# First attention in pairs of heads, with one 512-column bias product per head and the outputs split between two engines

## The chip, the cores and the metric

One core of a Trainium2 chip runs the whole program. The metric is the device time of one execution in microseconds (us); the kernel before took 2679.9 us (median of three runs, 2677.56 to 2681.17). The engines named here: TensorE (PE in the profile, PEld for its weight loads) multiplies into eight PSUM banks; VectorE (DVE), ScalarE (ACT) and GpSimd (POOL) do elementwise work; SyncE (SP) issues DMAs. Each engine works through its own queue in order and waits on semaphores.

## The reference, cut to what matters

The program is a transformer block (`first_block`) followed by two layers of another kind. Only the attention part of `first_block` is touched. It has 8 MoBA heads of 64 (with 256 tokens there is one block, so this is causal attention), 8 sliding-window heads of 64 that share 2 key/value heads, and 4 memory heads of 128:

```
s = q @ k.T * scale + bias_table[h, bucket(qpos - kpos)]      # MoBA and window heads
s = where(allowed, s, -inf)
p = exp(s - max(s)); p = p / (sum(p) [+ exp(sink - max)])     # the sink only for window heads
o = p @ v                                                     # 256 tokens x 64 (or 128)
merged = sigmoid(g_mb)*(o_mb @ w_branch_moba) + sigmoid(g_sw)*(o_sw @ w_branch_swa) + sigmoid(g_me)*(o_me @ w_branch_mem)
```

Memory heads have no bias and no mask. Everything is float32.

## The kernel before, in words

**A split-product kernel.** Every weight matrix is streamed by DMA in blocks into `raw` (two buffers), split by ACT into `w_hi` and by POOL (line 749) into `w_lo`, and used by PE (line 1934) in three products, hi by hi, hi by lo and lo by hi. Each of these buffers has two slots, so the split of a block waits until PE has used up the block two before it. Activations too are kept as a rounded part and a rest (`u_hi`/`u_lo`, `o1_hi`/`o1_lo`).

**The first attention** (step `att1` of the plan) runs over 20 units `UNITS1`: 8 MoBA heads, 8 window heads, 4 memory heads. A unit's scores are 256 queries by 256 keys and lie in one PSUM bank: queries 0..127 in columns 0..255 (`qb` 0), queries 128..255 in the others. The bias and the mask come from `hank`, a table in SBUF of 384 columns per head; a product of the reversed identity `reverse` with a 256-column window of it adds the biases of one half of the queries.

Each engine has its own loop over steps n, with lags between the parts of a unit (`T_LAG` = 3, `O_LAG` = 4). They are ordered like this:

- PE: `scores1(n)` (lines 2262 and 2266: for each `qb` a score product, then a bias product), `transposes1(n-3)` (line 2275), `outputs1(n-4)` (line 2291).
- DVE: `max1(n)` (line 1611, then 1614 and 1615 for window heads or 1617, which frees the exponentials by `nmax_ready`), `probs1(n-1)` (lines 1625, 1626, 1631), `out1(n-5)` (line 1647 copies the output from PSUM to `work`, 1649 rounds it into `o1_hi`, 1650 takes the rest into `o1_lo`).
- ACT: `copy_pt1(n-3)` (line 1103), `exp1(n)` (line 1093 for the sink, line 1095 for the two halves).

Score banks are 0, 1 and 6; transposes use 2 and 3, outputs 4 and 5. Bank 7 is not used here, only later for the modulation. `claim` and the counts in `plan.add("att1", ...)` make PE wait until a bank has been read `taken[b]` times. `v_sw` holds the values of both window key/value heads side by side, and since an output product computes 128 rows, of which 64 are used, `out1` picks the rows and moves them to the place that the head needs.

When the last output product has been issued, PE goes on with the three branch projections (line 1934), whose first blocks are split already.

Of the kernel before, what the change touches and what calls it, by code (L numbers as in the profile page):

```python
# [126 lines left out]
class Gemm:  # L127


    def __init__(self, plan, name, src, blocks, per, kt, cols, gpb, banks, mod=0, mod_bodies=None, acc=0, whole=False,  # L130
                 shift=None, token_major=False, counted=True, uses=1, late=None):
        self.token_major = token_major
        self.late = late
        self.name, self.src, self.kt, self.cols = name, src, kt, cols
        self.per, self.bodies, self.gpb, self.banks = per, blocks // per, gpb, banks
        self.blocks = blocks
        self.first = plan.total.get("blk", 0)
        self.g0 = plan.total.get("grp", 0)
# [6 lines left out]
        self.n_pairs = mod * len(self.mod_bodies) - (1 if shift and mod == 2 else 0)  # L145
        self.shift_turn, self.shift_step = plan.total.get("turn", 0), self.first_step + PAIR_STEPS * self.n_pairs
# [4 lines left out]
        counts["turn"] = 1 if shift else 0  # L151
        counts["mod_steps"] = PAIR_STEPS * self.n_pairs + KD * self.shift_halves
# [38 lines left out]
def make_plan(a):  # L191
# [44 lines left out]
    plan.add("att1", b0=7, b1=7, b6=6, b2=10, b3=10, b4=10, b5=10)  # L236
# [8 lines left out]
    plan.add("mod_00", turn=1)  # L245
# [4 lines left out]
    for l in range(LAYERS):  # L250
# [9 lines left out]
        plan.add(f"mod_{l}1", turn=1)  # L260
# [17 lines left out]
        plan.add(f"mod_{l}2", turn=1)  # L278
# [4 lines left out]
        if not last:  # L283
            plan.add(f"mod_{l + 1}0", turn=1)
# [15 lines left out]
def two_blocks(nc, a, out):  # L300
# [7 lines left out]
    with ctx:  # L308
# [56 lines left out]
        v_sw = sb("v_sw", [P, 2, P], on=a1)  # L365
# [140 lines left out]
        o_done = sem("o_done")  # L506
        o_ready = sem("o_ready")
# [9 lines left out]
        SCORE1 = (0, 1, 6)  # L517
# [270 lines left out]
        def _(act):  # L788
# [282 lines left out]
            def kv_sw(st, i, c):  # L1071

                act.wait_ge(group_done, st.done(0, 1))
                for kv in range(2):
                    for to in range(2):
                        ins = act.activation(k_sw[64 * to:64 * to + 64, kv, :], bank[0][64 * kv:64 * kv + 64, 0:S], ACT.Copy)
                ins.then_inc(taken[0], 1)
                act.wait_ge(group_done, st.done(0, 2))
                act.activation(v_sw[:, :, :], bank[1][:, 0:2 * P].rearrange("p (t n) -> p t n", t=2), ACT.Copy) \
                   .then_inc(taken[1], 1)  # L1080
# [4 lines left out]
            def exp1(n):  # L1085
                kind, h = UNITS1[n]
                scale = 0.125 if kind != "mem" else 1.0 / math.sqrt(128)
                act.wait_ge(nmax_ready, n + 1)
                if n >= 2:
                    act.wait_ge(prob_ready, n - 1)  # L1090
                st_ = stat[:, n % 2, :]
                if kind == "swa":
                    act.activation(st_[:, 6:8], st_[:, 2:4], ACT.Exp, bias=sinks[:, h:h + 1])
                for q in range(2):
                    ins = act.activation(work[:, n % 2, q * S:(q + 1) * S], bank[SCORE1[n % 3]][:, q * S:(q + 1) * S], ACT.Exp,
                                         bias=st_[:, 2 + q:3 + q], scale=scale, accum_out=st_[:, 4 + q:5 + q])
                ins.then_inc(taken[SCORE1[n % 3]], 1)
# [8 lines left out]
            for n in range(len(UNITS1) + T_LAG):  # L1106
                if n >= T_LAG:
                    copy_pt1(n - T_LAG)
                if n < len(UNITS1):
                    exp1(n)  # L1110
# [180 lines left out]
        def _(dve):  # L1291
# [105 lines left out]
            def late_norm(name, st, late_tile):  # L1397

                sc0, turn = plan.at(name, "scaled"), before_joint(name).shift_turn

                def take_shift():
                    dve.wait_ge(mod_done, turn + 2)
                    hs = late_halves(name)
                    hs = slice(hs[0], hs[-1] + 1)
                    dve.tensor_reduce(shift[:, :, hs], bank[7][:, :].rearrange("p (t h n) -> p t h n", t=2, h=2)[:, :, hs],
                                      AX.X, ALU.add).then_inc(taken[7], 1)
                    dve.wait_ge(taken[7], turn + 2)
# [198 lines left out]
            def max1(n):  # L1606
# [4 lines left out]
                link(dve.tensor_reduce(st_[:, 0:2], bank[SCORE1[n % 3]][:, :].rearrange("p (q k) -> p q k", q=2), AX.X, ALU.max))  # L1611
# [7 lines left out]
            def probs1(n):  # L1619
                kind, h = UNITS1[n]  # L1620
                b = SCORE1[n % 3]
                dve.wait_ge(taken[b], plan.at("att1", f"b{b}") + n // 3 + 1)
# [11 lines left out]
            def out1(n):  # L1634
                kind, h = UNITS1[n]
                b = 4 + n % 2
                dve.wait_ge(o_done, n + 1)
                if kind == "moba":
                    tile, to, of, w = h // 2, 64 * (h % 2), 64 * (h % 2), 64
                elif kind == "swa":  # L1640
                    tile, to, of, w = 4 + h // 2, 64 * (h % 2), 64 * (h // 4), 64
                else:
                    tile, to, of, w = 8 + h, 0, 0, P
                if n >= 2:
                    dve.wait_ge(o_ready, n - 1)
                src = work[to:to + w, 2 + n % 2, 0:S]
                dve.tensor_copy(src, bank[b][of:of + w, 0:S]).then_inc(taken[b], 1)
                dve.wait_ge(taken[b], plan.at("att1", f"b{b}") + n // 2 + 1)
                link(dve.tensor_copy(o1_hi[to:to + w, tile, :], src))
                dve.tensor_tensor(o1_lo[to:to + w, tile, :], src, o1_hi[to:to + w, tile, :].bitcast(f32), ALU.subtract) \  # L1650
                   .then_inc(o_ready, 1)
# [61 lines left out]
            def modulation(l, i):  # L1713
# [9 lines left out]
                dve.wait_ge(taken[7], turn + 2)  # L1723
# [199 lines left out]
        def _(pe):  # L1923
# [16 lines left out]
            def modulate(l, i):  # L1940
# [3 lines left out]
                pe.wait_ge(taken[7], plan.at(step, "turn") + 1)  # L1944
# [6 lines left out]
            def add_shift(name):  # L1951

                old = before_joint(name)
                pe.wait_ge(taken[7], old.shift_turn + 1)
# [293 lines left out]
            def scores1(n):  # L2248
                kind, h = UNITS1[n]
                b = SCORE1[n % 3]  # L2250
                claim("att1", b, n // 3)
                if kind == "moba":
                    r = slice(64 * (h % 2), 64 * (h % 2) + 64)
                    q, k, table = qk_mb[r, h // 2, :], qk_mb[r, 4 + h // 2, :], h
                elif kind == "swa":
                    r = slice(64 * (h % 2), 64 * (h % 2) + 64)
                    q, k, table = q_sw[r, h // 2, :], k_sw[r, h // 4, :], 8 + h
                else:
                    q, k, table = q_me[:, h, :], k_me[:, h, :], None
                for qb in range(2):  # L2260
                    dst = bank[b][:, qb * S:(qb + 1) * S]
                    ins = pe.matmul(dst, q[:, qb * P:(qb + 1) * P], k, start=True, stop=table is None)
                    if table is not None:

                        shift = P * (1 - qb)
                        ins = pe.matmul(dst, reverse, hank[:, table, shift:shift + S], start=False, stop=True)
                ins.then_inc(score_ready, 1)

            def transposes1(n):
# [3 lines left out]
                for kt in range(2):  # L2273
                    for qb in range(2):
                        ins = pe.transpose(bank[b][:, kt * S + qb * P:kt * S + (qb + 1) * P],
                                           probs[:, n % 2, qb * S + kt * P:qb * S + (kt + 1) * P], ident)
                ins.then_inc(pt_done, 1)

            def outputs1(n):
# [20 lines left out]
            for n in range(n_units + O_LAG):  # L2300
                if n < n_units:
                    scores1(n)
# [63 lines left out]
            def layer(l):  # L2366
# [117 lines left out]
                def outputs(n):  # L2484
# [4 lines left out]
                    if n == 1:  # L2489
                        pe.wait_ge(taken[7], plan.at(f"att_{l}", "turn") + 1)  # L2490
# [91 lines left out]
```

## Time and profile before

| what | value |
|---|---|
| median of three runs | 2679.9 us |
| the profiled execution: its own time, its span | 2680.03 us, 2678.2 us |
| PE busy | 2579.2 us (96%) |
| DVE, ACT, POOL busy | 52%, 40%, 49% |
| granted TensorE clock, mean | 0.986 of full speed |
| first attention, on PE | from 141.8 to 216.0 us |

Busy time of PE includes modelled ends of pipelined products, so 96% does not mean that every product runs at full rate. The time between the starts of two consecutive products tells what one costs. Lines such as L1934 are lines of helpers that serve many stages, so a stage is read by its window of time.

### The profile page before, as it was taken

What the parts mean: (1) busy time and instruction counts of PE and PEld (TensorE: products, weight loads), DVE (VectorE), ACT (ScalarE), POOL (GpSimd) and SP (SyncE); (2) the same over time, 40 slices, a digit from 0 to 9 for tenths busy, and PEclk for the clock granted to TensorE, in tenths of its full rate; (3) what the DMA queues carried; (4) which work ended last, traced back from release to release, by engine and by line L of the source; (5) the groups of instructions that cost most, each with busy time, mean ns of one, the idle gap of its engine ahead of it and who ended that gap; (6) DMA issues with size and microseconds to landing.
All of it is one profiled execution on the core that took longest, in us unless ns stands there. A gap on an engine that the chain in (4) does not pass through costs nothing.

```text
span 2678.2 us, 42499 instructions
## 1 busy us (share of the span) xinstructions
PE 2579.2 (96%) x14948; PEld 2241.7 (84%) x14948; DVE 1398.8 (52%) x3175; ACT 1069.1 (40%) x1934; POOL 1307.3 (49%) x654
## 2 busy tenths in 40 slices
PE   7998999989999999999999999999999999999997
PEld 7967999978888888867788888888888888789997
DVE  3665755455556662355477555665554453546221
ACT  4444457433332342166534222342222342565442
POOL 4615868754444444233344444444444453456875
PEclk9999989999999999999999999999999999999998
DMA  6704745654444543121233443544444452324553
GB/s 197 229 24 158 241 137 188 184 162 136 146 141 133 162 143 126 40 71 64 76 102 125 150 151 120 171 128 156 141 136 118 138 188 77 97 95 142 188 165 118
DMA packets 414007, 365.88 MB, mean 137 GB/s; under 512 B 7484, under 2 KB 412558, under 8 KB 413888
## 3 DMA queue, kind: packets, MB, share of 16 engines
q1 hardware_dynamic: 411448, 359.14, 42.6%
q10 hardware_dynamic: 2440, 5.16, 0.6%
q8 instruction: 74, 1.21, 0.2%
q14 instruction: 45, 0.37, 0.0%
HBM read 363.19 MB, written 1.08 MB: 136 GB/s over the span
## 4 chain that ended last, share of the span: by engine, by line
PE 69%; issue 14%; POOL 13%; DVE 2%; ACT 2%; DMA 0%; POOLq 0%; SPq 0%; ACTq 0%; DVEq 0%
PE bank L1934 58%; POOL w_lo L749 13%; PE bank L2454 2%; PE bank L2020 1%; PE bank L2494 1%; PE bank L2021 1%; PE bank L2025 1%; PE bank L2398 1%; DVE stat L1840 1%; PE bank L2120 1%; PE bank L2390 1%; PE bank L2146 0%; PE bank L2480 0%; PE bank L2147 0%; PE bank L2151 0%
## 5 line engine op out<-in xcount | busy, mean ns | idle before, releaser
L749 POOL TENSOR_TENSOR w_lo<-raw,w_hi 128x1024 fp32r<-128x1024 f32 (+2 forms) x602 | 1280.7, 2141 | 1268.3 <-ACT w_hi L820 809.0
L1934 PE MATMUL bank<-u_hi,w_hi 128*128 128x512 f32 (+1 forms) x2456 | 835.6, 340 | 8.5 <-POOL w_lo L749 4.5
L1934 PE MATMUL bank<-u_lo,w_hi 128*128 128x512 f32 (+1 forms) x2456 | 830.3, 338 | 0.0
L1934 PE MATMUL bank<-u_hi,w_lo 128*128 128x512 f32 (+1 forms) x2456 | 830.0, 338 | 0.0
L820 ACT ACTIVATE w_hi<-raw 128x1024 fp32r<-128x1024 f32 (+3 forms) x392 | 366.2, 949 | 881.7 <-PE bank L1934 693.2
L1934 PEld LDWEIGHTS bank<-u_hi,w_hi 128*128 128x128 f32 x2456 | 468.6, 191 | 79.9 <-issue 27.9
L1934 PEld LDWEIGHTS bank<-u_hi,w_lo 128*128 128x128 f32 x2456 | 468.5, 191 | 48.9
L1934 PEld LDWEIGHTS bank<-u_lo,w_hi 128*128 128x128 f32 x2456 | 468.7, 191 | 48.0
L1447 DVE SCALAR_TENSOR_TENSOR bank<-mod_raw,cond,bank 128x256 f32<-128x256 f32 x1008 | 401.3, 483 | 0.1
L1934 PE MATMUL bank<-hid_hi,w_hi 128*128 128x512 f32 (+1 forms) x880 | 308.6, 351 | 19.1 <-POOL w_lo L749 18.9
L1934 PE MATMUL bank<-hid_hi,w_lo 128*128 128x512 f32 (+1 forms) x880 | 306.3, 348 | 0.0
L1934 PE MATMUL bank<-hid_lo,w_hi 128*128 128x512 f32 (+1 forms) x880 | 306.3, 348 | 0.0
L1735 DVE TENSOR_TENSOR bank<-bank,work 128x512 f32<-128x512 f32 (+1 forms) x88 | 55.7, 633 | 366.1 <-PE bank L1934 355.0
L809 ACT ACTIVATE w_hi<-raw 128x1024 fp32r<-128x1024 f32 (+3 forms) x142 | 129.8, 953 | 193.8 <-PE bank L1934 142.0
L1934 PEld LDWEIGHTS bank<-hid_hi,w_hi 128*128 128x128 f32 x880 | 168.1, 191 | 42.5 <-POOL w_lo L749 12.5
L1934 PEld LDWEIGHTS bank<-hid_hi,w_lo 128*128 128x128 f32 x880 | 167.9, 191 | 20.8
L1934 PEld LDWEIGHTS bank<-hid_lo,w_hi 128*128 128x128 f32 x880 | 168.1, 191 | 20.5
L1934 PE MATMUL bank<-w_hi,u_hi 128*128 128x256 f32 (+1 forms) x432 | 131.6, 305 | 0.7 <-POOL w_lo L749 0.7
L1443 DVE TENSOR_SCALAR bank<-mod_raw,cond 128x256 f32<-128x256 f32 x144 | 62.6, 480 | 121.5 <-DMA mod_raw<-in_w_mod 120.9
L1934 PE MATMUL bank<-w_hi,u_lo 128*128 128x256 f32 (+1 forms) x432 | 123.2, 285 | 0.0
L1934 PE MATMUL bank<-w_lo,u_hi 128*128 128x256 f32 (+1 forms) x432 | 123.1, 285 | 0.0
L1758 DVE SCALAR_TENSOR_TENSOR x<-bank,mod_g,x 128x256 f32 (+1 forms) x80 | 35.6, 479 | 136.2 <-PE bank L1934 127.3
(271 smaller groups left out, 3401.9 us busy)
## 6 DMA issues: line engine op xcount, KB each, us to landing
raw<-in_ffn_w_in SPq DMA_DIRECT2D x88, 1024.0 KB, 5.1
mod_raw<-in_w_mod SPq DMA_DIRECT2D x144, 512.0 KB, 4.5
raw<-in_w_in SPq DMA_DIRECT2D x67, 1024.0 KB, 5.2
raw<-in_ffn_w_out SPq DMA_DIRECT2D x64, 704.0 KB, 4.7
raw<-in_w_ffn_up SPq DMA_DIRECT2D x22, 1024.0 KB, 5.1
raw<-in_w_ffn_down SPq DMA_DIRECT2D x16, 704.0 KB, 4.8
raw<-in_w_attn_out SPq DMA_DIRECT2D x8, 1024.0 KB, 5.2
raw<-in_w_o SPq DMA_DIRECT2D x8, 1024.0 KB, 5.2
```

The lines of the kernel that those rows point to most:

```text
L749: pool.tensor_tensor(st.half(t, w_lo[slot]), st.half(t, raw[slot]), st.half(t, w_hi[slot]).bitcast(f32), ALU.subtract).then_inc(lo_ready, 1)
L809: act.activation(st.half(t, w_hi[s % 2]), st.half(t, raw[s % 2]), ACT.Copy).then_inc(hi_ready, 1)
L820: act.activation(st.half(t, w_hi[n % 2]), st.half(t, raw[n % 2]), ACT.Copy).then_inc(hi_ready, 1)
L1443: ins = dve.tensor_scalar(so_far, value, by(k, h), None, ALU.mult)
L1447: ins = dve.scalar_tensor_tensor(dst, value, by(k, h), so_far, ALU.mult, ALU.add)
L1735: dve.tensor_tensor(prod, prod, work[:, t, 0:w], ALU.mult).then_inc(hid_prod, 1)
L1758: ins = dve.scalar_tensor_tensor(cols, bank[t][:, lo:lo + S].rearrange("p (o t) -> p o t", o=1), mod_g[:, i_mod, at, h], cols, ALU.mult, A ...
L1840: link(dve.tensor_reduce(st_[:, c:c + 1], bank[score_bank(n, c)][:, 0:nk], AX.X, ALU.max))
L1934: ins = pe.matmul(dst, s, v, start=first and n == 0, stop=final and n == 2)
L2020: pe.matmul(bank[2 * c + t][:, 0:width], w_hi[slot][:, w], m_hi(k), start=k == 0, stop=False)
L2021: pe.matmul(bank[2 * c + t][:, 0:width], w_lo[slot][:, w], m_hi(k), start=False, stop=False)
L2454: ins = pe.matmul(bank[score_bank(n, c)][:, 0:nk], q2[r, h, at:at + P], k2[r, h, 0:nk], start=True, stop=True)
```

## The change

The scores of two heads (units 2m and 2m+1) are issued together in every second step of PE. Each head with a bias gets one product of 512 columns, which reads two overlapping windows of `hank`, ahead of its score products. The four score products then alternate between the two heads; for heads of 64 these lie in partitions 0..63 and 64..127. The halves of the queries change places in the bank. There are four score banks (7 is added), and later users of bank 7 count its releases separately (`b7`). The output is no longer copied to `work`: ACT writes its rounded part from PSUM to `o1_hi`, at the head of its step, and DVE takes the rest from PSUM, at the head of its step, ahead of the maximum of the new scores. `v_sw` is kept twice, the second time with its two heads exchanged, and each window head takes the one in which its rows already lie where the output goes.

```diff
-    plan.add("att1", b0=7, b1=7, b6=6, b2=10, b3=10, b4=10, b5=10)
+    plan.add("att1", b0=5, b1=5, b6=5, b7=5, b2=10, b3=10)
...
-        SCORE1 = (0, 1, 6)
+        SCORE1 = (0, 1, 6, 7)
+        def out_place(n):
+
+            kind, h = UNITS1[n]
+            if kind == "mem":
+                return slice(0, P), 8 + h
+            return slice(64 * (h % 2), 64 * (h % 2) + 64), (0 if kind == "moba" else 4) + h // 2
...
 ACT, kv_sw
-                act.activation(v_sw[:, :, :], bank[1][:, 0:2 * P].rearrange("p (t n) -> p t n", t=2), ACT.Copy) \
-                   .then_inc(taken[1], 1)
+                values = bank[1][:, 0:2 * P].rearrange("p (t n) -> p t n", t=2)
+                act.activation(v_sw[:, 0, :, :], values, ACT.Copy)
+                act.activation(v_sw[:, 1, :, 0:64], values[:, :, 64:P], ACT.Copy)
+                act.activation(v_sw[:, 1, :, 64:P], values[:, :, 0:64], ACT.Copy).then_inc(taken[1], 1)
...
 ACT, first attention
-            for n in range(len(UNITS1) + T_LAG):
-                if n >= T_LAG:
+            def out_hi1(n):
+                rows, tile = out_place(n)
+                act.wait_ge(o_done, n + 1)
+                act.activation(o1_hi[rows, tile, :], bank[4 + n % 2][rows, 0:S], ACT.Copy).then_inc(o_part, 1)
+
+            for n in range(len(UNITS1) + O_LAG + 1):
+                if n >= O_LAG + 1:
+                    out_hi1(n - O_LAG - 1)
+                if T_LAG <= n < len(UNITS1) + T_LAG:
                     copy_pt1(n - T_LAG)
                 if n < len(UNITS1):
                     exp1(n)
...
 DVE, out1: the copy to work, the wait and the rounding are gone
+                rows, tile = out_place(n)
+                dve.wait_ge(o_part, n + 1)
+                dve.tensor_tensor(o1_lo[rows, tile, :], bank[4 + n % 2][rows, 0:S], o1_hi[rows, tile, :].bitcast(f32), ALU.subtract) \
                    .then_inc(o_ready, 1)
...
             for n in range(n_units + O_LAG + 1):
+                if n >= O_LAG + 1:
+                    out1(n - O_LAG - 1)
                 if n < n_units:
                     max1(n)
                 if 1 <= n <= n_units:
                     probs1(n - 1)
-                if n >= O_LAG + 1:
-                    out1(n - O_LAG - 1)
...
 PE
+            def scores1(pair):
+
+                for n in pair:
+                    kind, h = UNITS1[n]
+                    b = SCORE1[n % 4]
...
+                    if kind != "mem":
+
+                        table = hank[:, h if kind == "moba" else 8 + h, 0:S]
+                        windows = bass.AP(tensor=table.tensor, offset=table.offset, ap=[list(table.ap[0]), [P, 2], [1, S]])
+                        pe.matmul(bank[b][:, :].rearrange("p (q k) -> p q k", q=2), reverse, windows, start=True, stop=False)
+                for qb in (1, 0):
+                    for n in pair:
...
+                        ins = pe.matmul(bank[SCORE1[n % 4]][:, (1 - qb) * S:(2 - qb) * S], q[:, qb * P:(qb + 1) * P], k,
+                                        start=kind == "mem", stop=kind == "mem" or qb == 0)
+                        if qb == 0:
+                            ins.then_inc(score_ready, 1)
...
 PE, outputs1
-                claim("att1", b, n // 2)
+                if n >= 2:
+                    pe.wait_ge(o_ready, n - 1)
+                else:
+                    claim("att1", b)
...
-                        v = v_sw[:, kt, :]
+                        v = v_sw[:, (h // 4 + h) % 2, kt, :]
...
             for n in range(n_units + O_LAG):
-                if n < n_units:
-                    scores1(n)
+                if n < n_units and n % 2 == 0:
+                    scores1((n, n + 1))
```

## Rows read from the trace of the kernel before

**Rows 1.** Windows: window, length, busy us (count) per engine, PEclk, DMA share, GB/s.
```profile
141.80:198.00 56.20, 56.19 (x229) 33.49 (x230) 36.99 (x119) 25.85 (x83) 2.49 (x2) 1.00 0.04 10
198.00:216.00 18.00, 14.74 (x77) 11.67 (x76) 16.75 (x53) 9.08 (x28) 0.00 (x0) 1.00 0.00 0
```
**Rows 2.** Timeline, one step of PE: start, length, engine, line, operation, [idle before, releaser].
```profile
186.57 0.70 PE L2262 MATMUL bank<-k_sw,q_sw 64*128 64x256 f32 x2
...
188.45 0.70 PE L2266 MATMUL bank<-tok,const 128*128 128x256 f32 x2
...
188.99 0.60 PE L2275 MATMUL bank<-const,root 128*128 128x128 f32 x4
...
189.43 1.03 PE L2291 MATMUL bank<-xn,v_sw 128*128 128x256 f32 x4
...
190.38 0.70 PE L2262 MATMUL bank<-k_sw,q_sw 64*128 64x256 f32 x2
```
**Rows 3.** Timeline, window head, DVE and ACT from the maximum to the exponential.
```profile
189.19 0.69 DVE L1611 TENSOR_REDUCE stat<-bank 128x2 f32<-128x512 f32 x1 [0.50 <-PE bank L2266]
...
190.18 0.17 DVE L1615 TENSOR_SCALAR stat<-stat 128x2 f32<-128x2 f32 x1
...
190.38 0.30 ACT L1093 ACTIVATE stat<-stat,sinks 128x2 f32<-128x2 f32 x1 [0.16 <-DVE stat L1615]
...
190.58 0.45 ACT L1095 ACTIVATE work<-bank,stat 128x256 f32<-128x256 f32 x1
```
**Rows 4.** Timeline, memory heads, DVE and ACT.
```profile
200.62 0.17 DVE L1617 TENSOR_SCALAR stat<-stat 128x2 f32<-128x2 f32 x1
...
200.82 0.47 ACT L1095 ACTIVATE work<-bank,stat 128x256 f32<-128x256 f32 x1 [0.81 <-DVE stat L1617]
...
201.79 0.60 ACT L1103 ACTIVATE xn<-bank 128x512 f32<-128x512 f32 x1
...
202.51 0.42 DVE L1650 TENSOR_TENSOR o_lo<-work,o_hi 64x256 fp32r<-64x256 f32 x1
202.96 0.69 DVE L1611 TENSOR_REDUCE stat<-bank 128x2 f32<-128x512 f32 x1
...
203.69 0.17 DVE L1617 TENSOR_SCALAR stat<-stat 128x2 f32<-128x2 f32 x1
```
**Rows 5.** Timeline, a norm: ACT rounds out of PSUM, DVE takes the rest.
```profile
57.79 0.78 ACT L952 ACTIVATE u_hi<-bank 128x256 fp32r<-128x256 f32 x2 [1.42 <-DVE bank L1335]
58.21 0.43 DVE L1324 TENSOR_TENSOR u_lo<-bank,u_hi 128x256 fp32r<-128x256 f32 x1
```
**Rows 6.** Timeline, the later attention: score products of two half-heads, then the next product.
```profile
1301.14 1.13 PE L2454 MATMUL bank<-k,q 64*128 64x512 f32 x4
1302.20 0.50 PE L1934 MATMUL bank<-u_hi,w_hi 128*128 128x512 f32 x1
...
1306.76 0.70 PE L2454 MATMUL bank<-k,q 64*128 64x256 f32 x4
1307.40 0.50 PE L1934 MATMUL bank<-u_hi,w_hi 128*128 128x512 f32 x1
```
**Rows 7.** Timeline, two float32 products of 512 columns with 128 rows.
```profile
1069.92 1.88 PE L2398 MATMUL bank<-tabs,f 128*128 128x512 f32 x4
```
**Rows 8.** Timeline, first score product, last maximum's scaling, first branch product.
```profile
141.81 0.67 PE L2262 MATMUL bank<-qk_mb 64*128 64x256 f32 x2 [0.74 <-issue]
...
209.45 0.17 DVE L1617 TENSOR_SCALAR stat<-stat 128x2 f32<-128x2 f32 x1
...
216.01 0.47 PE L1934 MATMUL bank<-o_hi,w_hi 128*128 128x256 f32 x1
```
**Rows 9.** Timeline, the first weight split after the first attention.
```profile
218.59 2.67 POOL L749 TENSOR_TENSOR w_lo<-raw,w_hi 128x512 fp32r<-128x512 f32 x2 [74.01 <-ACT w_hi L820]
```
**Rows 10.** Timeline, the split of the last block of `q_me`.
```profile
130.96 4.77 POOL L749 TENSOR_TENSOR w_lo<-raw,w_hi 128x1024 fp32r<-128x1024 f32 x2 [3.48 <-ACT w_hi L809]
```
**Rows 11.** Windows, a stretch of the third branch projection.
```profile
252.00:264.00 12.00, 7.47 (x46) 7.27 (x45) 3.67 (x10) 5.01 (x8) 7.64 (x5) 0.76 0.86 275
```

More of the change, by code:

```diff
@@ L145, in __init__ @@
         self.n_pairs = mod * len(self.mod_bodies) - (1 if shift and mod == 2 else 0)
+        self.shift_b7 = plan.total.get("b7", 0)
         self.shift_turn, self.shift_step = plan.total.get("turn", 0), self.first_step + PAIR_STEPS * self.n_pairs
@@ L151, in __init__ @@
         counts["turn"] = 1 if shift else 0
+        counts["b7"] = 1 if shift else 0
         counts["mod_steps"] = PAIR_STEPS * self.n_pairs + KD * self.shift_halves
@@ L244, in make_plan @@
     gemm("up1", pairs(a["w_ffn_up"][0]), 22)
-    plan.add("mod_00", turn=1)
+    plan.add("mod_00", turn=1, b7=1)
     gemm("down1", down(a["w_ffn_down"][0]), 16, per=4, kt=DOWN_KT, cols=P, banks=(0, 1), mod=1,
@@ L259, in make_plan @@
         gemm(f"up_{l}0", pairs(a["ffn_w_in_2"][l, 0]), 22, mod=1, mod_bodies=range(1, 11), banks=(0, 1), **first)
-        plan.add(f"mod_{l}1", turn=1)
+        plan.add(f"mod_{l}1", turn=1, b7=1)
         gemm(f"down_{l}0", down(a["ffn_w_out_2"][l, 0]), 16, per=4, kt=DOWN_KT, cols=P, banks=(0, 1),
@@ L277, in make_plan @@
         gemm(f"attn_out_{l}", cols(a["w_attn_out_2"][l], 0), 4, mod=0 if last else 1, counted=False)
-        plan.add(f"mod_{l}2", turn=1)
+        plan.add(f"mod_{l}2", turn=1, b7=1)
         gemm(f"w_o_{l}", cols(a["w_o_2"][l], 0), 4, acc=4, whole=True, shift=(f"n2_{l}", halves))
@@ L283, in make_plan @@
         if not last:
-            plan.add(f"mod_{l + 1}0", turn=1)
+            plan.add(f"mod_{l + 1}0", turn=1, b7=1)
         gemm(f"down_{l}1", down(a["ffn_w_out_2"][l, 1]), 16, per=4, kt=DOWN_KT, cols=P, banks=(0, 1),
@@ L364, in two_blocks @@
         k_sw = sb("k_sw", [P, 2, S], on=a1)
-        v_sw = sb("v_sw", [P, 2, P], on=a1)
+        v_sw = sb("v_sw", [P, 2, 2, P], on=a1)
         q_me = sb("q_me", [P, 4, S], on=a1)
@@ L506, in two_blocks @@
         o_done = sem("o_done")
+        o_part = sem("o_part")
         o_ready = sem("o_ready")
@@ L1094, in exp1 @@
                 for q in range(2):
-                    ins = act.activation(work[:, n % 2, q * S:(q + 1) * S], bank[SCORE1[n % 3]][:, q * S:(q + 1) * S], ACT.Exp,
+                    ins = act.activation(work[:, n % 2, q * S:(q + 1) * S], bank[SCORE1[n % 4]][:, q * S:(q + 1) * S], ACT.Exp,
                                          bias=st_[:, 2 + q:3 + q], scale=scale, accum_out=st_[:, 4 + q:5 + q])
-                ins.then_inc(taken[SCORE1[n % 3]], 1)
+                ins.then_inc(taken[SCORE1[n % 4]], 1)
             def copy_pt1(n):
@@ L1397, in late_norm @@
             def late_norm(name, st, late_tile):
-                sc0, turn = plan.at(name, "scaled"), before_joint(name).shift_turn
+                sc0, turn, used = plan.at(name, "scaled"), before_joint(name).shift_turn, before_joint(name).shift_b7
                 def take_shift():
@@ L1406, in take_shift @@
                                       AX.X, ALU.add).then_inc(taken[7], 1)
-                    dve.wait_ge(taken[7], turn + 2)
+                    dve.wait_ge(taken[7], used + 2)
                 def scale(t):
@@ L1610, in max1 @@
                 st_ = stat[:, n % 2, :]
-                link(dve.tensor_reduce(st_[:, 0:2], bank[SCORE1[n % 3]][:, :].rearrange("p (q k) -> p q k", q=2), AX.X, ALU.max))
+                link(dve.tensor_reduce(st_[:, 0:2], bank[SCORE1[n % 4]][:, :].rearrange("p (q k) -> p q k", q=2), AX.X, ALU.max))
                 if kind == "swa":
@@ L1620, in probs1 @@
                 kind, h = UNITS1[n]
-                b = SCORE1[n % 3]
-                dve.wait_ge(taken[b], plan.at("att1", f"b{b}") + n // 3 + 1)
+                b = SCORE1[n % 4]
+                dve.wait_ge(taken[b], plan.at("att1", f"b{b}") + n // 4 + (2 if b == 7 else 1))
                 st_ = stat[:, n % 2, :]
@@ L1634, in out1 @@
             def out1(n):
[L1635 to L1650, printed above, removed]
+                rows, tile = out_place(n)
+                dve.wait_ge(o_part, n + 1)
+                dve.tensor_tensor(o1_lo[rows, tile, :], bank[4 + n % 2][rows, 0:S], o1_hi[rows, tile, :].bitcast(f32), ALU.subtract) \
                    .then_inc(o_ready, 1)
@@ L1722, in modulation @@
                 ins.then_inc(taken[7], 1)
-                dve.wait_ge(taken[7], turn + 2)
+                dve.wait_ge(taken[7], plan.at(f"mod_{l}{i}", "b7") + 2)
                 for h in range(2):
@@ L1943, in modulate @@
                 part = mod_part[:, i * n * 16:(i + 1) * n * 16].rearrange("p (n h t b) -> p b n t h", h=2, t=2, b=4)
-                pe.wait_ge(taken[7], plan.at(step, "turn") + 1)
+                pe.wait_ge(taken[7], plan.at(step, "b7") + 1)
                 pe.wait_ge(mod_step, plan.at(step, "mod_steps"))
@@ L1953, in add_shift @@
                 old = before_joint(name)
-                pe.wait_ge(taken[7], old.shift_turn + 1)
+                pe.wait_ge(taken[7], old.shift_b7 + 1)
                 pe.wait_ge(mod_step, old.shift_step + KD * old.shift_halves)
@@ L2246, in _ @@
             gemm("q_me", features(*u_of(x_cols), S))
[L2248 to L2267, printed above, removed]
+            def scores1(pair):
+                for n in pair:
+                    kind, h = UNITS1[n]
+                    b = SCORE1[n % 4]
+                    if b == 7:
+                        pe.wait_ge(taken[7], plan.at("att1", "b7") + n // 4 + 1)
+                    else:
+                        claim("att1", b, n // 4)
+                    if kind != "mem":
[4 more added lines that the diff above has]
+                    for n in pair:
+                        kind, h = UNITS1[n]
+                        if kind == "moba":
+                            r = slice(64 * (h % 2), 64 * (h % 2) + 64)
+                            q, k = qk_mb[r, h // 2, :], qk_mb[r, 4 + h // 2, :]
+                        elif kind == "swa":
+                            r = slice(64 * (h % 2), 64 * (h % 2) + 64)
+                            q, k = q_sw[r, h // 2, :], k_sw[r, h // 4, :]
+                        else:
+                            q, k = q_me[:, h, :], k_me[:, h, :]
+                        ins = pe.matmul(bank[SCORE1[n % 4]][:, (1 - qb) * S:(2 - qb) * S], q[:, qb * P:(qb + 1) * P], k,
+                                        start=kind == "mem", stop=kind == "mem" or qb == 0)
+                        if qb == 0:
+                            ins.then_inc(score_ready, 1)
@@ L2275, in transposes1 @@
                         ins = pe.transpose(bank[b][:, kt * S + qb * P:kt * S + (qb + 1) * P],
-                                           probs[:, n % 2, qb * S + kt * P:qb * S + (kt + 1) * P], ident)
+                                           probs[:, n % 2, (1 - qb) * S + kt * P:(1 - qb) * S + (kt + 1) * P], ident)
                 ins.then_inc(pt_done, 1)
@@ L2282, in outputs1 @@
                 pe.wait_ge(taken[2 + n % 2], plan.at("att1", f"b{2 + n % 2}") + n // 2 + 1)
-                claim("att1", b, n // 2)
+                if n >= 2:
+                    pe.wait_ge(o_ready, n - 1)
+                else:
+                    claim("att1", b)
                 for kt in range(2):
@@ L2489, in outputs @@
                     if n == 1:
-                        pe.wait_ge(taken[7], plan.at(f"att_{l}", "turn") + 1)
+                        pe.wait_ge(taken[7], plan.at(f"att_{l}", "b7") + 1)
                     elif n >= 2:
```

## The prediction

> **What bounds the kernel now.** I read the windows of the first attention first, since nothing else is touched. Up to 198 us PE is busy without a gap at a clock of 1.00, while DVE is busy for two thirds and ACT for less than half of the time; from 198 us on, in the memory heads, PE has gaps (14.74 of 18 us) and DVE is the full engine, with 16.75 of 18 us [rows 1]. The timeline of one step then gives the period: 3.81 us from one unit's scores to the next's (186.57 to 190.38), of which the transposes take 0.44 and the two output products 0.95 [rows 2]. The memory heads' sequence shows the other loop, the maximum and its scaling, the exponentials, then what follows [rows 4]. The whole part lasts 74.2 us, from 141.8 to 216.0 [rows 8]: three units at 2.51 us (scores alone), thirteen with transposes and most with outputs at up to 3.81, four DVE-bound at 2.9, and the tail. Behind it the weight supply begins anew: POOL had been idle for 74.01 us when PE's first branch block freed a slot [rows 9]. So the supply gets nothing done while attention runs, and whatever attention saves should shift all that follows.
>
> **What a product costs.** Two products of 512 columns take 1.88 us with about 0.17 of modelled end, so 0.85 each [rows 7]; 256 columns are then 0.43. A step of PE holds six products of 256 columns (2.56) and four transposes (0.44), together 3.0, and lasts 3.81. The missing 0.81 goes to its four changes between 64-row and 128-row products, 0.2 each: the last bias product, which is followed by another 128-row operation, takes 0.54, and the others about 0.63 [rows 2].
>
> **Two heads at once.** The later attention issues the scores of two half-heads in opposite halves of the rows. With 512 columns both together take 1.06 us, with 256 columns 0.64 [rows 6]. The difference, 0.42, is what 256 columns cost once, not twice: the two run side by side, and 0.21 is fixed. The new order issues a, b, a, b of 256 columns each; if it behaves as 512 columns do, that is 1.06 for all four. The other end, all four one after another, is 4 x 0.43 + 0.2 = 1.9. I take 1.06, because the row is of the same form with the same number of columns per half. What the row does not show is a second product in the same half.
>
> The Trainium skill bears on that (TensorE: Matmul & The Clock Gate, Part 3: a weight load overlaps a running product only where it goes to another row group). By that rule the second product of a half would wait with its load for the first; at about 0.1 us for each of four loads (a transpose goes by in 0.11 with its load) the pair would cost 0.4 more, an estimate that, over five pairs, would end 2 us later than my sum. No row here separates the two, and the sum goes without it.
>
> **PE after.** A pair of heads of 64: two bias products 1.71, four scores 1.06, change back 0.2, so 2.97; two sets of transposes and outputs 2.78. That is 5.75; counting bare columns (5.15) and two changes gives 5.56. I take 5.7 per pair, 2.85 per unit, against 3.81. The bias product reads two overlapping windows instead of one run; its ends are 0.85 and, at half rate, 1.7. I take 0.85, the row of 512 columns.
>
> **DVE and ACT after.** DVE loses the copy and the rounding; ACT gains one rounding out of PSUM. A norm has the very pair: ACT's rounding starts, DVE's rest starts 0.42 later and takes 0.43 [rows 5]. But the new order makes a loop. In DVE's queue the rest of unit n-5 stands before the maximum of unit n, and it needs ACT's rounding, which stands in ACT's queue behind the exponentials of unit n-1, which need the scaling of n-1. Going round once, from scaling to scaling: to the exponential 0.20, to the next operation of ACT 0.97 (200.62, 200.82, 201.79), to DVE's rest 0.42 [rows 5], to the maximum 0.45, to the scaling 0.73 (202.51, 202.96, 203.69) [rows 4]. Sum 2.77. A window head adds the sink's exponential, 0.20 (190.38 to 190.58), and one more DVE operation: 0.99 instead of 0.73 from maximum to scaling (189.19 to 190.18) [rows 3]. Sum 3.23. DVE's reciprocal and probabilities and ACT's copy of transposes fall into gaps of the loop. PE's outputs are in time for it: within a pair at PE's pace the output of n-4 ends 0.6 us before ACT comes to it. If that slack went, its shortfall would be added once per pair.
>
> So MoBA units go at PE's 2.85 (the loop is right behind at 2.77), window units at the loop's 3.23 with PE waiting, and memory units, whose PE work is only 2.3, at 2.77 instead of 2.9.
>
> **The sum.** Scores of pair 0 from 141.8 to 144.8, pair 1 to 147.7. The first transposes need the first probabilities: scaling 145.7, exponentials to 146.9, probabilities to 147.8, so they are issued at once after pair 1. Pair 2 goes from 148.2 to 151.2, pair 3 starts at 154.0, pair 4 (first window heads) at 159.6 and ends at 162.6. Its first scaling is at 162.6 + 0.2 + 0.99 = 163.8. Seven rounds of 3.23 and one of 2.97 (to the first memory head) give 189.4, three of 2.77 give 197.7 for the last scaling, which was at 209.45 [rows 8]. The tail: DVE's and ACT's remaining rounds let the last transposes go 3.2 us later, their copy ends at 4.35, the last output product at 5.4. The branch starts at 203.1 instead of 216.0: 12.9 us saved, of which some 4.6 come from MoBA, 5.5 from window heads and the rest from memory heads and tail.
>
> The two extra copies for `v_sw`, at most 0.38 each by the size of [rows 5], delay ACT's next split and so POOL's by under 0.8 us. POOL is done with that block at 135.7 [rows 10]; the last of PE's groups, 24 products of 0.12 us, starts 2.9 us before the scores, at about 138.2. I cost them at nothing; uncovered they are 0.8. Counting bank 7 apart costs nothing: nobody else uses it in this part.
>
> The profiled execution took 2680.0 us, 0.1 from the median. Forecast: 2680.0 - 12.9 = 2667.1 us, rounded to 2667.
>
> **The rivals.**
> (a) The scores of a pair don't overlap (1.9 instead of 1.06). PE needs 3.28 per unit, which replaces the loop as bound in window heads too. Against the sum: pairs 0 and 1 end 1.7 later, three more pairs before the first window scaling add 2.6, the window heads 0.4: the end is 4.7 later, 2672. For it: no row has four in a row. Against it: [rows 6].
> (b) The loop does not bind in window heads, because ACT or DVE reach the next operation sooner than the rows say; then these go at 2.85: 8 x 0.38 = 3 us less, 2664. Against it: queues are in order, and each term is a measured distance.
> (c) The bias window is read at half rate: 1.7 more per pair, 3.7 per unit. Nothing would be left of MoBA's and the window heads' gain: 2679 to 2680.
> (d) The gain is made but given back: the branch and gate stages wait for weights (PE busy 7.47 of 12 us in [rows 11], with DMA at 0.86). If that supply ran on during attention, a shorter attention would only lengthen the waits: 2680. Against it: the 74 us of idle POOL [rows 9] and 0 to 0.04 DMA [rows 1].
> (e) Slower: the clock. PE now has gaps in every window unit (0.4 of 3.23 us). In the stretch with 62% busy PE the granted clock was 0.76 [rows 11], so it had been at its lower level of half speed for part of it. If it fell with the first window pair, PE's work per window unit doubles to 5.6 and per memory unit to 4.5: 8 x 2.4 + 4 x 1.7 = 26 more, less 12.9: 2693. Against it: the memory heads before kept 1.00 at 82% busy [rows 1]; the new window heads are at 88%, the memory heads at 83%. It decides if the clock falls for more than half of the 40 us.
>
> **How the numbers follow.** The sum as it is 0.73; (a), in full or part, 0.12; (b) 0.05; (c) 0.03; (d) 0.04; (e) 0.03. Ends of unknown costs and places where the later stages' waits and clock fall differently after a shift add 2 us either way. The range from 2662 to 2674 holds the sum, (a) and (b). A change of under 0.2% (5.4 us) can't be told from none here: faster by more has 0.92 (the sum, (a), (b), and a part of (c) and (d)), within it 0.05, slower 0.03.
>
> **What would show it.** In the profile after: two starts of 512-column bias products 0.85 apart; the four score products of a pair within about 1.1 us (1.9 would be rival a); scores of successive MoBA pairs 5.7 us apart, of window pairs 6.5, of memory pairs 5.5; DVE idle before its rest, released by ACT's rounding, in nearly every step; the first branch product at 203; the same length as before behind it. Wrong would be a bias product of 1.7, a clock under 1.00 between 160 and 203, a first branch product at 203 with an end that has not moved, or window heads that PE bounds.

## The result, and the profile after

The changed kernel took 2663.87 us (median of 4), the kernel before 2678.73: 0.9945 of it, 95% interval 0.9932 to 0.9957. The forecast was 2667. In a second comparison on one chip it was 0.9939 (0.9923 to 0.9956). The profiled executions took 2664.12 and 2680.03 us. All medians and ratios here leave out two executions of a later run, out_only, which took 4197.7 and 4602.31 us at granted clocks of 0.56 and 0.76.

The first branch product ends the first attention, as in [rows 8]. The timeline of the changed kernel:

```profile
141.76 1.96 PE L2267 MATMUL bank<-tok,const 128*128 128x512 f32 x4 [0.74 <-issue]
...
201.54 0.47 PE L1940 MATMUL bank<-o_hi,w_hi 128*128 128x256 f32 x1
...
204.13 2.67 POOL L759 TENSOR_TENSOR w_lo<-raw,w_hi 128x512 fp32r<-128x512 f32 x2 [59.60 <-ACT w_hi L830]
```

The part lasts 59.78 us instead of 74.20, 14.4 less. POOL's idle time ahead of its first split is 59.60 us where it was 74.01 [rows 9]: shorter by the same 14.4, so the supply starts when PE frees a slot, and the saving is not given back behind it: from the first branch product to the end of the span it is 2460.8 us, before 2462.2. That the rest is 1.4 us shorter too is scatter, since over the profiles of the table below, all with the same code there, it lies between 2459.0 and 2462.8.

The two extra copies of `v_sw` stand ahead of the part. It starts at 141.76 us, before at 141.81, so they show no cost, but later runs move this start by up to 5 us, and the 0.8 us that the prediction names would not be seen in that.

MoBA heads, one pair of PE's steps (timeline, engine PE; L2267 bias, L2279 scores, L2290 transposes, L2309 outputs; a float32 product leaves two records, so x8 are four products):

```profile
153.76 1.88 PE L2267 MATMUL bank<-tok,const 128*128 128x512 f32 x4
...
155.57 1.14 PE L2279 MATMUL bank<-qk_mb 64*128 64x256 f32 x8
...
156.64 0.66 PE L2290 MATMUL bank<-const,root 128*128 128x128 f32 x4
...
157.13 1.03 PE L2309 MATMUL bank<-xn,v_mb 128*128 128x256 f32 x4
...
158.00 0.60 PE L2290 MATMUL bank<-const,root 128*128 128x128 f32 x4
...
158.44 1.03 PE L2309 MATMUL bank<-xn,v_mb 128*128 128x256 f32 x4
...
159.30 1.88 PE L2267 MATMUL bank<-tok,const 128*128 128x512 f32 x4
```

Two bias products take 1.81 us (153.76 to 155.57), the four score products 1.07, the pair 5.54; two heads took 7.62 [rows 2]. PE has no gap there. In the window heads it goes on issuing scores at nearly the same pace, and is held back mainly in the memory heads (timeline, the score products of pairs 5, 6, 7 and 9):

```profile
166.65 1.14 PE L2279 MATMUL bank<-k_sw,q_sw 64*128 64x256 f32 x8
...
172.18 1.14 PE L2279 MATMUL bank<-k_sw,q_sw 64*128 64x256 f32 x8
...
177.86 1.14 PE L2279 MATMUL bank<-k_sw,q_sw 64*128 64x256 f32 x8
...
188.66 1.89 PE L2279 MATMUL bank<-y,q_me 128*128 128x256 f32 x8
```

What sets the pace from the first window head on are DVE and ACT, which fall behind PE's scores. This is the forecast loop, in the changed kernel's timeline of DVE and ACT (to be read against [rows 3, 4, 5]):

```profile
175.89 0.17 DVE L1634 TENSOR_SCALAR stat<-stat 128x2 f32<-128x2 f32 x1
...
176.09 0.30 ACT L1105 ACTIVATE stat<-stat,sinks 128x2 f32<-128x2 f32 x1 [1.06 <-DVE stat L1634]
...
177.19 0.37 ACT L1121 ACTIVATE o_hi<-bank 64x256 fp32r<-64x256 f32 x1
...
177.59 0.42 DVE L1656 TENSOR_TENSOR o_lo<-bank,o_hi 64x256 fp32r<-64x256 f32 x1 [0.62 <-ACT o_hi L1121]
...
177.93 0.67 DVE L1630 TENSOR_REDUCE stat<-bank 128x2 f32<-128x512 f32 x1
...
178.90 0.17 DVE L1634 TENSOR_SCALAR stat<-stat 128x2 f32<-128x2 f32 x1
```

DVE finishes a scaling at 175.89, waits for ACT's rounding of an old output, and only then may take the maximum whose scores have long been in their bank. The next scaling is at 178.90. The one before was at 172.60: rounds of 3.29 and 3.01 us alternate, 3.15 on average. The views of waits say the same: over the part, DVE's rest waited 12.8 us for ACT in 18 places. PE's own waits, apart from 0.7 us at its start, were these, and all but one stand in the memory heads and the tail:

```profile
PE bank L2309 <- ACT xn L1115: 3.1, 5, 0.7
PE bank L2290 <- DVE root L1650: 1.5, 3, 0.8
```

The windows of the three kinds of heads, to be read like [rows 1], have the clock at 1.00 throughout; PE is full in the first, lacks 0.5 us in the second and has its gaps in the third:

```profile
141.76:160.90 19.14, 19.14 (x88) 11.12 (x88) 12.47 (x40) 12.87 (x42) 2.49 (x2) 1.00 0.09 29
160.90:182.20 21.30, 20.80 (x109) 14.03 (x109) 15.20 (x52) 13.85 (x47) 0.00 (x0) 1.00 0.00 1
182.20:201.54 19.34, 15.30 (x78) 11.54 (x77) 13.30 (x45) 13.76 (x43) 0.00 (x0) 1.00 0.00 0
```

Where the 14.4 us come from can be read at DVE's scalings. The first one of the window heads comes 7.8 us sooner (163.28 against 171.12), from there to the first one of the memory heads it takes 24.95 us instead of 29.50, from there to the last one 7.98 instead of 8.83, and the tail behind it 5.33 instead of 6.56. The first scaling of the window heads (timelines of DVE, the kernel before and the changed one):

```profile
171.12 0.17 DVE L1615 TENSOR_SCALAR stat<-stat 128x2 f32<-128x2 f32 x1
...
163.28 0.17 DVE L1634 TENSOR_SCALAR stat<-stat 128x2 f32<-128x2 f32 x1
```

### The profile page after: what moved, and what is told of

The parts are those of the page before. It is cut to its first block, busy times and chain, and to the rows that moved or that the text cites. A ratio compares the mean times of both kernels' runs of the same rounds, so it can differ in the third digit from the quotient of the medians.

```text
span 2662.3 us, 42401 instructions
## 1 busy us (share of the span) xinstructions
PE 2564.8 (96%) x14916; PEld 2235.2 (84%) x14916; DVE 1385.8 (52%) x3135; ACT 1075.7 (40%) x1956; POOL 1307.6 (49%) x654
## 4 chain that ended last, share of the span: by engine, by line
PE 69%; issue 13%; POOL 13%; DVE 3%; ACT 2%; POOLq 0%; DMA 0%; SPq 0%; ACTq 0%; DVEq 0%
PE bank L1940 58%; POOL w_lo L759 13%; PE bank L2472 2%; PE bank L2026 1%; PE bank L2512 1%; PE bank L2027 1%; PE bank L2031 1%; PE bank L2416 1%; DVE stat L1846 1%; PE bank L2126 1%; PE bank L2408 1%; PE bank L2152 0%; PE bank L2498 0%; PE bank L2153 0%; PE bank L2157 0%
```

## The experiments

Where the part starts differs from run to run (138.4 to 143.7 us among the runs below, with the same code ahead of it), and that alone moves a whole execution by some us. The part itself repeats to 0.02 us. So "part" below is the time from the first product of the first attention to the first branch product, read from each profile; before it is 74.20, changed 59.78. Beside it stands the median where a kernel was executed several times, else the one time, which says little beside a scatter of some us.

| run | part, us | median, us (ratio to before) |
|---|---|---|
| pairs_only | 63.22 | 2666.92 (0.9952, 0.9936 to 0.9968) |
| out_only_b | 72.32 | one run: 2674.27; out_only, median of nine: 2675.64 (0.999, 0.998 to 1.000) |
| single_bias_first | 65.41 | one run: 2668.84 |
| same_half | 64.42 | one run: 2667.33 |
| one_head_then_other | 59.80 | one run: 2660.91 |
| bias_256 | 59.81 | one run: 2668.16 |
| out_last | 59.16 | 2664.05 (0.9943, 0.9930 to 0.9957) |
| out_mid | 55.11 | 2656.99 (0.9917, 0.9904 to 0.9931) |
| changed_again | 59.79 | 2663.01 (0.9939, 0.9923 to 0.9956) |
| out_mid_again | 55.12 | 2657.78 (0.9915, 0.9898 to 0.9931) |

**pairs_only.** The new scores with the old output path (the edit is cut to its place in DVE's step; the comments say what else differs).

```diff
-                if n >= O_LAG + 1:
-                    out1(n - O_LAG - 1)       # o_hi by ACT, rest by DVE, first in the step
+                if n >= O_LAG + 1:
+                    out1(n - O_LAG - 1)       # copy, rounding and rest by DVE, last in the step
```

> The PE side of the change alone: pairs of heads, 512-column bias products, four score banks; outputs are taken by DVE alone in its old three operations at the end of its step. Theory: PE's 2.77 us is then covered by DVE's own sum, 2.87 us a unit in MoBA and memory heads and about 3.2 in window heads; last scaling at 197.8, first branch product at 204.4 us, that is 11.6 of the 14.5 us. Rival (the split of the output is what frees the kernel, and pairs alone leave the step at DVE's pace near the old 3.8): first branch product after 210.

The first branch product came 63.2 us into the part (expected 62.6). The PE side alone gives 11.0 of the 14.4 us. Window units go at 3.3 us, near DVE's own sum: DVE's timeline shows no wait there. One wait I had not listed: PE's output products, nearly always the second of a pair, wait for DVE to empty their bank (nine such waits, 7.8 us). One of them:

```profile
178.90 1.10 PE L2317 MATMUL bank<-xn,v_sw 128*128 128x256 f32 x4 [0.82 <-DVE work L1664]
```

**out_only and out_only_b.** The new output path with the old scores, one head a step (the body of `scores1` is cut).

```diff
-                if n < n_units and n % 2 == 0:
-                    scores1((n, n + 1))
+                if n < n_units:
+                    scores1(n)                # score, bias, score, bias of 256 columns
```

> The DVE and ACT side of the change alone: outputs rounded by ACT and taken by DVE ahead of the new scores, v_sw kept twice, but the scores of one head a step with the old four products in turn (in the new banks and halves). Theory: PE's 3.81 us a unit still bounds MoBA and window heads, only the memory heads and the tail gain; first branch product at 213.2 us, 2.8 us less than before. Rival (DVE work was on the path): 3.2 us a unit and a first branch product near 206.

> Output side alone once more, for a profile at full clock: as told for out_only, first branch product at 213.2 us if the output work was off the path before, near 206 if it was on it.

The part is read from the second, the median from the first. It lasts 72.32 us, 1.9 less than before (2.8 expected), all in the memory heads and the tail. MoBA and window heads kept 3.81 us to the hundredth. So DVE's old output work was off the path while PE had four changes a head. 11.0 and 1.9 make 12.9; the other 1.5 appear only with both.

**single_bias_first.** One head a step, in the new order.

```diff
-                if n < n_units and n % 2 == 0:
-                    scores1((n, n + 1))
+                if n < n_units:
+                    scores1((n,))
```

> The changed kernel with the scores of one head in each step instead of a pair in every second: one 512-column bias product, then the two score products, which lie in the same half of the rows. It tells the two parts of the new score order apart. Theory: two changes between 64 and 128 rows instead of four (0.2 each) and no running side by side: 3.33 us a unit against 3.81 before and 2.77 in pairs; first branch product at 205.6 us. Rival (64-row float32 products cost half anyway and need no partner in the other half): 2.9 us a unit, then ACT's and DVE's loop bounds, first branch product near 202.

```profile
161.23 1.13 PE L2279 MATMUL bank<-qk_mb 64*128 64x256 f32 x4
162.28 0.66 PE L2290 MATMUL bank<-const,root 128*128 128x128 f32 x4
162.78 1.03 PE L2309 MATMUL bank<-xn,v_mb 128*128 128x256 f32 x4
163.65 1.02 PE L2267 MATMUL bank<-tok,const 128*128 128x512 f32 x2
164.60 1.13 PE L2279 MATMUL bank<-k_sw,q_sw 64*128 64x256 f32 x4
```

3.37 us a unit (3.33 expected); two score products in one half take 1.05 us (161.23 to 162.28), the same as four in both halves. Two changes between 64-row and 128-row products instead of four take a unit from 3.81 to 3.37. What the pair adds to that, from 3.37 to 2.77, same_half divides.

**same_half.** Both heads of a pair in the same half.

```diff
-        UNITS1 = [("moba", h) for h in range(8)] + [("swa", h) for h in range(8)] + [("mem", h) for h in range(4)]
+        UNITS1 = [(kind, h) for kind in ("moba", "swa") for h in (0, 2, 1, 3, 4, 6, 5, 7)] + [("mem", h) for h in range(4)]
```

> The changed kernel with the heads in the order 0, 2, 1, 3, 4, 6, 5, 7, so that both heads of a pair lie in the same half of the rows. Theory (the two halves run side by side and only that halves the time): the four score products of a pair take 1.9 us instead of 1.06, MoBA pairs 6.4 instead of 5.54, window pairs 6.4, first branch product 206 us. Rival (a 64-row product is cheap by itself): 1.06 us and 201.5. It also shows where the alternation of ACT's and DVE's distances (exponential to rounding 0.90 and 1.02 us, rest to maximum 0.34 and 0.46) comes from: with the rows of the output it changes every second unit here, with the number of the bank or unit every unit as before.

```profile
157.36 1.99 PE L2279 MATMUL bank<-qk_mb 64*128 64x256 f32 x8
159.29 0.33 PE L2290 MATMUL bank<-const,root 128*128 128x128 f32 x1
```

The same eight records take 1.93 us instead of 1.07; the pair takes 6.40 (155.55 to 161.95), the part 64.42. That four products cost the time of two is the work of the two halves. A unit takes 3.20 us here. So of the 1.04 us that PE saves per unit, 0.44 come from two changes fewer, 0.17 from one more (a pair needs two where two single heads need four), and 0.43 from the halves running side by side.

**one_head_then_other.**

```diff
-                for qb in (1, 0):
-                    for n in pair:
+                for n in pair:
+                    for qb in (1, 0):
```

> The changed kernel with the four score products of a pair in the order a, a, b, b instead of a, b, a, b. Theory (products in opposite halves run side by side, but start in order): the second product of a and the first of b overlap, the four take 1.5 us instead of 1.06, MoBA pairs 5.97 us instead of 5.54, first branch product at about 203.5 us, all of it lost before the window heads. Rival (the time of a pair comes from fewer changes between 64 and 128 rows only, not from running side by side): the same 1.06 us and 201.5.

The expectation fell: 59.80 and 1.07 us (153.34 to 154.41). Read from later and later times, the timeline of this run counts down its eight records by twos (the three lines are of three such readings):

```profile
153.34 1.14 PE L2279 MATMUL bank<-qk_mb 64*128 64x256 f32 x8
...
153.66 0.82 PE L2279 MATMUL bank<-qk_mb 64*128 64x256 f32 x6
...
153.88 0.60 PE L2279 MATMUL bank<-qk_mb 64*128 64x256 f32 x4
```

Two records start together each time, in this order too. The rival (only fewer changes) is refuted by same_half. What was wrong in the theory is its second half: products did not have to start in the program's order when the next one had the other half to itself. The records don't name the head, but records of one half start 0.22 us apart, so two that start together are of both heads. The alternation in the code is not what pays.

**bias_256.** Each head's bias in two products of 256 columns.

```diff
-                        pe.matmul(bank[b][:, :].rearrange("p (q k) -> p q k", q=2), reverse, windows, start=True, stop=False)
+                        for half in range(2):
+                            pe.matmul(bank[b][:, half * S:(half + 1) * S], reverse,
+                                      hank[:, h if kind == "moba" else 8 + h, half * P:half * P + S], start=half == 0, stop=False)
```

> The changed kernel with each head's 512-column bias product issued as two of 256 columns, one after the other, still ahead of the score products. Theory (columns cost, not instructions: 0.43 per 256, and it is the grouping of 128-row products that saves, not their width): nothing changes, 5.54 us per MoBA pair, 59.8 us from the first product to the first branch product. Rival (the wide product itself saves): each extra instruction costs 0.1 us or more, MoBA pairs 5.75 us, 60.5 us or more.

59.81: no difference. The 512-column product named in the change saves nothing by its width; that both biases stand together ahead of the scores does.

**out_last.** The rest of an old output behind the probabilities, as before.

```diff
                 if 1 <= n <= n_units:
                     probs1(n - 1)
+                if n >= O_LAG + 1:
+                    out1(n - O_LAG - 1)       # taken away from the head of the step
```

> The changed kernel with one edit: DVE takes the rest of an old output (out1) at the end of its step, behind the maximum and the probabilities, as the kernel before did. Theory (a loop through ACT and DVE bounds the window and memory heads: scaling, exponentials, rounding of an old output, its rest, next maximum, 3.15 us a unit in window heads, 2.72 in memory heads): with the rest behind the maximum the loop is cut, window units fall to PE's 2.77 and memory units to about 2.25, the first branch product comes at 197 instead of 201.5 us, and the kernel takes 4 to 5 us less than the changed one (about 2659.5 us). Rival (PE or DVE's own sum bounds them, and the order does not matter): first branch product at 201.5, no change. Rival (the old place makes PE's output products wait for the bank): later than 201.5.

Missed: 59.16, not 55.3. The loop is cut, DVE's rest waits only 2.2 us for ACT (12.8 in the changed kernel), memory heads go at 2.32 us; but window pairs take 6.59 us, and the reason is the second rival:

```profile
173.19 1.10 PE L2309 MATMUL bank<-xn,v_mb 128*128 128x256 f32 x4 [0.82 <-DVE o_lo L1656]
```

There are two output banks. The second output product of a pair needs the bank that DVE reads at the end of its step, and PE is there 0.8 us too soon. That closes another loop, since the maximum, which stands ahead of the rest in DVE's step, waits for PE's scores of the next pair:

```profile
177.10 0.69 DVE L1630 TENSOR_REDUCE stat<-bank 128x2 f32<-128x512 f32 x1 [1.63 <-PE bank L2279]
```

So taking the output ahead, as the change does, removes one wait and makes another of nearly the same price.

**out_mid, changed_again, out_mid_again.**

```diff
                 if n < n_units:
                     max1(n)
+                if n >= O_LAG + 1:
+                    out1(n - O_LAG - 1)
                 if 1 <= n <= n_units:
                     probs1(n - 1)
```

> The changed kernel with one edit: DVE takes the rest of an old output between the maximum of the new scores (with its scaling) and the probabilities. At the head of the step (the changed kernel) a loop through ACT bounds window heads at 3.15 us; at the end of the step (out_last) the second output product of a pair waited 0.8 us for its bank. Theory: in the middle both go, since the bank is free 0.6 to 0.8 us sooner than at the end and the maximum stands ahead of the wait for ACT: window pairs at PE's 5.54 to 5.7 us instead of 6.3, memory pairs 4.5 instead of 5.4, first branch product at 197 us (the changed one's 201.5), whole kernel 4.5 us less than the changed one. Rival (the probabilities, now behind ACT's rounding, come late for the transposes and PE waits there): 6 us or more per pair and 200 to 202 us.

> The changed kernel as it is, beside out_mid_again on the same chip. All theories: 59.8 us for the first attention; 14 to 15 us less than before.

> out_mid once more, beside the changed kernel on the same chip. Theory: 55.1 us for the first attention, 4.7 us less than the changed kernel in the part and in the whole. Rival (part of the 7 us between the medians of the earlier calls is lost or gained in later stages): the whole differs by clearly more or less than 4.7.

55.11 and 55.12 against 59.78 and 59.79. Both waits nearly go: DVE's rest waits 1.8 us for ACT, PE's outputs 0.7 us for DVE. The windows of out_mid show PE full through the window heads and nearly so in the memory heads:

```profile
142.14:161.40 19.26, 19.26 (x88) 11.11 (x88) 12.72 (x40) 13.33 (x44) 2.49 (x2) 1.00 0.09 29
161.40:183.00 21.60, 21.60 (x112) 14.76 (x112) 17.05 (x56) 15.25 (x51) 0.00 (x0) 1.00 0.00 0
183.00:197.25 14.25, 13.46 (x74) 11.13 (x74) 11.69 (x40) 11.60 (x36) 0.00 (x0) 1.00 0.01 2
```

Window pairs take 5.68 us. On the same chip the medians are 5.2 us apart (2663.01 and 2657.78), about the 4.7 of the part, and the four executions of one don't overlap with the four of the other. This version beats both kernels.

## Why the prediction was right, and where its sizes were off

- **Bound and place.** PE up to 198 us, the cost of its changes between 64-row and 128-row products (0.44 us a unit for two fewer, in single_bias_first), and the supply that stands still: right. Rival (d) is out by POOL's 59.60.
- **Scores of a pair, 1.06.** Measured 1.07; rival (a) is out, and same_half is what (a) would have looked like (its 1.9 is 1.93 there, and its 4.7 us in all are 4.64). The weight-load rule quoted from the Trainium skill (TensorE: Matmul & The Clock Gate, Part 3) would have added 0.4 per pair; the records of one half start 0.22 apart (153.66, 153.88), which is one record's own time (half of 0.43) and leaves no room for a load. In this form it does not hold.
- **Bias products, 0.85 each.** Measured 1.81 for the two with the change behind them (1.71 and 0.1); reading two overlapping windows costs nothing beside plain runs of 256 columns (bias_256: 59.81), rival (c) is out.
- **PE's pair, 5.7.** Mis-sized: 5.54. I had two counts, 5.56 by columns and changes and 5.75 with 0.95 for the outputs, and took a value between. The 0.95 already held part of the next change, which I added again. By the first scaling of the window heads (163.8 forecast, 163.28 measured) that is 0.5 us.
- **The loop, 3.23 and 2.77.** Right as a mechanism: out_last and out_mid cut it and DVE's waits for ACT fall from 12.8 to 2.2 and 1.8 us. Its size was 3.15 and 2.66, since every second round is 0.28 shorter (see the last section): 0.65 and 0.35 us. Rival (b) is out.
- **PE in the window heads.** Wrong, without a cost in the sum. The prediction had PE waiting in every window unit, scores of window pairs 6.5 us apart and PE 88% busy. Its scores stood 5.54, 5.54 and 5.68 us apart and it was busy for 20.80 of 21.30 us. With four score banks and transposes three units behind, PE ran ahead of a loop that takes 6.3 us a pair, and was held mainly in the memory heads, whose two pairs of scores came 4.5 and 6.3 us behind the pair before each, where 5.5 was forecast. The end follows the loop all the same, from scaling to scaling up to the last one at 196.21.
- **Where the gain lies.** The prediction gives 4.6 us to MoBA and 5.5 to the window heads; by its own scalings, with 171.12 for the first one before, it would have been 7.3 and 3.9. Measured: 7.8 and 4.6.
- **The tail, 5.4.** Measured 5.33 (196.21 to 201.54).
- **Sum.** 12.9 forecast, 14.4 measured in the part; the terms above, 0.5 + 0.65 + 0.35 + 0.07, make up the difference. All four erred to the same side. Between the medians it is 14.9, and what lies between that and 14.4 is within the scatter of the rest. The forecast of 2667 also started from an execution of 2680.0, 1.3 us above the median before.
- **Clock (e).** 1.00 in all three windows, at 79% busy too.
- **What I did not see.** The reason why the output has to be taken early, the two output banks. The prediction held that PE's outputs were in time and asked nowhere what DVE's order does to their banks; the same oversight made the expectation of out_last wrong, where it stood only as a rival.

## What to carry to other kernels

Group products by the rows that they use, and let the products of a group lie in opposite halves: here that was 11 of 14 us, some three fifths of a unit's saving by the grouping and the rest by the halves, and neither the width of the products nor the order within the group mattered. When a step of an in-order engine is moved, follow it both ways: whom it now waits for with everything behind it (here ACT, 3.15 us a unit), and who waits for what it frees (here PE, 0.8 us a pair); the best place may be between the two. A gap of the busiest engine need not stand where the loop binds: here DVE and ACT fell behind in the window heads, and PE waited mainly in the memory heads. Time the part that was changed in the profile when the rest of the kernel scatters more than the difference.

## What the runs showed of the hardware

- Two float32 products on 64 rows each, in opposite halves, run at the same time: their records start together, and four take 1.07 us against 1.93 in one half. They did so even when the code issued both of one head first. The Trainium skill (TensorE: Matmul & The Clock Gate, Part 3) says that products start strictly in order; the timeline of one_head_then_other, with two records starting at 153.34, 153.66 and 153.88, speaks against that across halves.
- The distances around an operation of ACT or DVE that takes 64x256 out of PSUM depend on the rows where it lies. Where no wait stands between, ACT's rounding starts 0.45 us after the second exponential if it lies in rows 0 to 63, and 0.58 if in rows 64 to 127; DVE's next operation starts 0.34 or 0.46 us after its rest. With heads in the order 0, 1, 2, 3 this alternates every unit, in same_half every second one (0.45, 0.45, 0.58, 0.58 and 0.34, 0.34, 0.46, 0.46), so it goes with the rows and not with the bank. It does not hold for every form: in the kernel before, where DVE's rest reads SBUF, one in rows 0 to 63 (205.39) was followed after 0.44 us. The cause was not tried.
